# Dilated branch: the first head's probabilities turned by VectorE squares and a trip through memory instead of by TensorE

## The chip, the cores and the metric

The kernel runs on one core of a Trainium2 chip. The metric is the device time of one execution in microseconds (us); lower is better.

## What is computed

A decoder layer over 1024 tokens of width 1024, in float32. One combined projection feeds three causal mixers (A: forgetting attention, B: sparse attention over the 256 keys that an indexer picks, C: dilated sliding-window attention) and their gates; a last projection, the residual and a norm follow. The change is in branch C:

```
C_GROUPS = ((128, 1), (512, 4), (2048, 16))     # window, dilation; 4 heads of 64 each
logits = q . k * 64**-0.5 - slope * dist         # keys t, t-d, t-2d, ...
lse = logsumexp(logits); p = exp(logits - lse)
o = einsum('bhqj,bqjhd->bqhd', p, v)             # then weighted by the groups' softmax shares
```

## The kernel before, in words

**One plan, five engines.** `build_plan` (line 71) writes one list of steps. Each engine walks the same list and does its part of each step, so the list is also the order of every engine's queue. Semaphores do the rest.

**Fill.** TensorE's time goes mostly to projections. A projection tile is 128 output columns by 1024 tokens; it has two banks of PSUM, bank 0 for tokens 0 to 511 and bank 1 for the rest, and its 8 input chunks come as two weight blocks of four. That makes four *pieces* of 12 matmuls (three for each chunk, since every float32 product is split in a high and a low part): first block into bank 0, first block into bank 1, second block into bank 0, second block into bank 1. After the third piece bank 0 is read out, after the fourth bank 1. The read-out of a q or k tile is one ACT instruction (line 1483, the high part) and then one VectorE instruction (line 1814, the low part), which frees the bank. For dilations 4 and 16 both go through a strided view. A v tile is read out by one VectorE transpose (line 1805). The next tile's first piece needs bank 0 free, its second piece bank 1. The weights are split in high and low two blocks ahead (ACT line 1355, VectorE line 1651), at the first piece of each block.

**Attention.** In branch C a channel is a pair of heads, a *run* is two blocks of 128 queries of one channel. There are 6 channels (two for each group) and 4 runs in each, so 24 runs, numbered 0 to 23 here, and *step* s of the loop in `pair_run` (line 241) is the one in which the logits of run s are made. A step of the plan does, in this order:

- TensorE: the logits of run s (line 1252); the product of probabilities and values ("pv", line 1291) of run s-2; the *turn* of run s-1 (line 1264), which transposes its probabilities in blocks of 128x128 through the identity, up to four blocks into a bank.
- VectorE: bias and row maximum of run s (line 1871). ACT: reads out pv (line 1554), copies the turned blocks from PSUM to the ring `pt` (line 1537), then does the exponentials of run s for both heads (line 1519).
- one bit of the selection that branch B needs later (`pick`, 24 bits within this stage): VectorE works out the next bit and does two counts ("bit", lines 1665 to 1678).
- 1.25 to 1.6 pieces of fill, with the read-out that they make due; then the other half of the counts ("bit_count": two by ACT, line 1560, two by VectorE), then as much fill again.

Banks 2 and 3 are handed out in turn to pv and to the groups of turned blocks. A run's blocks number 3 or 4 for each head in group one, 3 in group two, 2 in group three; a run with more than four blocks over both heads needs two groups, and the second one gets the bank that pv just used.

**Squares.** Branches A and B already turn part of the first head's blocks in another way: VectorE transposes the 32x32 squares inside each block in place (line 1792), ACT's queue stores the result to memory (line 1528), and GpSimd's queue loads it again in four DMAs that put the squares in their places (line 1036). pv then reads these blocks from `ptsa`, `ptsb` or `c_tables`. There ACT does the first head's exponentials in the step "square", before the second head's.

The fill follows a pattern of four steps for each channel. With the next channel's tiles q, k and v of four pieces each, the steps hold: (1st) q, q, q; (2nd) q, k, k; (3rd) k, k, v; (4th) v, v, v. Channel 0's fill and the last channel's differ a little.

Of the kernel before, what the change touches and what calls it, by code (L numbers as in the profile page):

```python
# [21 lines left out]
P = 128  # L22
# [3 lines left out]
TB = T // P  # L26
# [16 lines left out]
COL, at = {}, 0  # L43
# [10 lines left out]
SPL = 3  # L54
EARLY = 1
RATE_B = 0.84
SQUARED = {"a": 8, "b": 4}
LAG = {"a": 3, "b": 2}
PTS = {"c": 4, "a": 4, "b": 3}
RELUS = 3  # L60
IDX_BLOCKS = ((7,), (6,), (5,), (4,), (3, 2))
SHARES = 3
# [1 line left out]
NCH = {"a": 4, "b": 4, "c": 6}  # L64
# [6 lines left out]
def build_plan():  # L71
# [20 lines left out]
    def step(kind, **kw):  # L92
        plan.append((kind, kw))
        return kw
# [128 lines left out]
    def pair_run(runs, before, rate, behind_square={}):  # L223


        n = len(runs)
        br = runs[0][0]["br"]
        by_dma = [br == "b" and br in SQUARED or br == "a" and r[0]["ch"] + 1 < NCH["a"] and runs[s + 1][0]["ch"] + 1 < NCH["a"]
                  for s, r in enumerate(runs)]
        by_dma.append(False)  # L230
        for run, dma in zip(runs, by_dma):
            for x in run:
                x.update(dma=dma, moved={})

        def open_parts(r):

            own = sum(x["W"] // P for x in runs[r])
            return 2 * own - len(runs[r][0]["moved"]) if by_dma[r] else 16

        defer[0] = True  # L240
        for s in range(n + 2):
            for f in before.get(s, []):
                f()
            def logits():
                run, wide = runs[s], sum(x["W"] for x in runs[s])
                slots = 2 if wide > HALF else 1
                first_S, first_L, col = nxt("S", slots), nxt("L", 2 * len(run)), 0
                for k, x in enumerate(run):
                    x.update(slots=slots, S=first_S, L=[first_L + k, first_L + len(run) + k], col=col,
                             last=x is run[-1], run=run, held=runs[s - 1][0] if s else None)  # L250
                    col += x["W"]
                    units_seen.append(x)
                    plan.append(("logits", x))

            def turn(run, groups):
                for g in run[0]["groups"][groups]:
                    g.update(use=ring(), tp=nxt("tp"))
                    unit_of_tp.append(run[0])
                step("turn", unit=run[0], groups=groups)

            between = 1 <= s < n and runs[s - 1][0]["slots"] == 2 and open_parts(s - 1) > 8
            if s < n and not between:
                logits()
            due = [r for r in range(max(s - 3, 0), min(s, n)) if r + (LAG[br] if by_dma[r] and by_dma[r + 1] else 2) == s]
            for r in due:
                pv = ring()
                for x in runs[r]:
                    x["pv"] = pv
                    plan.append(("pv", x))

            def square():
                if not by_dma[s]:
                    return
                own = [(x["b"], 0, c) for x in runs[s] for c in range(x["W"] // P)]
                at = len(squares) - 2
                for x in runs[s]:
                    x.update(square=len(squares), single=sum(y["slots"] == 1 for y in squares),
                             moved={part: k for k, part in enumerate(own[:SQUARED[br]])})
                step("square", unit=runs[s][-1], n=len(squares), before=squares[at] if at >= 0 else None)
                squares.append(runs[s][-1])  # L280

            if s < n and not between:
                square()
            for f in behind_square.get(s, []):
                f()
            if 1 <= s <= n:
                moved = runs[s - 1][0]["moved"]
                parts = [(x["b"], hh, c) for x in runs[s - 1] for hh in range(2) for c in range(x["W"] // P)]
                parts = sorted((part for part in parts if part not in moved), key=lambda part: part[1] if moved else 0)
                groups = [dict(parts=parts[g0:g0 + 4]) for g0 in range(0, len(parts), 4)]  # L290
                for x in runs[s - 1]:
                    x["groups"] = groups
                if between:
                    turn(runs[s - 1], slice(0, 2))
                    logits()
                    square()
                    turn(runs[s - 1], slice(2, None))
                else:
                    turn(runs[s - 1], slice(0, None))
            if s == n and runs[0][0]["br"] != "c":  # L300
                step("share_inverse", br=runs[0][0]["br"])
            if s < n:
                plan.append(("exp", runs[s][-1]))
            x = runs[min(s, n - 1)][-1]
            many = len(runs[min(s, n - 1)])
            if s < n and x["br"] == "a" and x["ch"] == NCH["a"] - 1 and x["b"] in (5, 6):
                step("q_split", ch=0, half=x["b"] - 5)
            if s < n and x["br"] == "b" and x["ch"] and x["b"] == 1:
                step("q_split", ch=x["ch"], half=1)
            if s < n and x["br"] == "b" and x["ch"] + 1 < NCH["b"] and x["b"] == 6:  # L310
                step("q_split", ch=x["ch"] + 1, half=0)
            if x["br"] == "b" and s == 0:
                next(fill[0])
                owed[0] = 0.5
            elif x["br"] == "c" and s == n:
                pick(now=False)
                pump(1)
                flush_later()
                count_now()
            elif x["br"] != "b" and s >= n:  # L320
                pump(1 if s == n else 0)
            elif x["br"] == "a" and x["ch"] == NCH["a"] - 1:
                pump(0 if x["b"] == 4 else 1)
            elif x["br"] == "c" and x["ch"] in (0, NCH["c"] - 1):
                pick(now=False)
                pump(1.25 if x["ch"] == 0 else 1.375)
                flush_later()
                count_now()
                pump(1.25 if x["ch"] == 0 else 1.375)
            elif x["br"] == "c":  # L330
                pick(now=False)
                pump(2 * rate)
                flush_later()
                count_now()
                pump(2 * rate)
            else:
                pump(3 if s >= n else many * 2 * rate)
            flush_later()
        defer[0] = False
# [227 lines left out]
def hybrid_layer_kernel(nc, x, norm_g, w_in, b_forget, g_cq, w_uq, w_uq_idx, g_ckv, w_ukv, w_a, w_b, w_c, w_o, final_g,  # L567
# [3 lines left out]
    with ExitStack() as ctx:  # L571
# [55 lines left out]
        v_index = {(a["br"], a["ch"]): a["n"] for kind, a in plan if kind == "v_store"}  # L627
        PR = {"a": at(28, "pa", [P, 2, T]), "b": at(32, "pb", [P, 2, T])}
        PT = {br: at(k, f"pt{br}", [P, PTS[br], 4, P]) for br, k in (("c", 54), ("a", 36), ("b", 40))}
        PTQ = {"a": [at(k, f"ptsa{k}", [P, TB, P]) for k in (44, 76)], "b": [at(46, "ptsb", [P, 4, P])]}  # L630

        idle_out, ties = at(96, "idle_out", [P, T], BF16), at(96, "ties", [P, T], F16)
        idle_out8, state = at(71, "idle_out8", [P, 6 * P], U8), at(71.75, "state", [P, 10, PICKS], I32)
# [697 lines left out]
        def _(act):  # L1331
# [4 lines left out]
            def then(ins):  # L1336
                chain[0] += 1
                ins.then_inc(act_chain, 1)
                act.wait_ge(act_chain, chain[0])

            def split_high(upto):

                while done[0] < min(upto, len(blocks)):
# [20 lines left out]
            for kind, a in plan:  # L1364
# [119 lines left out]
                elif kind == "logits":  # L1484
                    if a["br"] == "c" and a["b"] == 0:
# [7 lines left out]
                        for hh in range(2):  # L1493
                            A(bmc[:, hh, 0:m.shape[1]], m, ACTF.Copy,
                              scale=float(np.float32(c_slope(2 * a["ch"] + hh)) * np.float32(C_GROUPS[g][1]))
                              ).then_inc(bias_ready, 1)
                elif kind == "square":
                    u = a["unit"]
                    if a["n"]:
                        act.wait_ge(square_stored, 16 * a["n"])  # L1500
# [8 lines left out]
                elif kind == "exp":  # L1509

                    if a["held"] is not None:
                        full(act, a["held"]["groups"][-1]["use"])
                        if a["held"]["dma"] and not a["dma"]:
                            act.wait_ge(square_stored, 16 * (a["held"]["square"] + 1))
                    for hh in range(1 if a["dma"] else 0, 2):
                        act.wait_ge(logit_ready, a["L"][hh] + 1)
                        for x in a["run"]:
                            mx, dn = stats_of(x, hh)
# [1 line left out]
                                    scale=-1.0, accum_out=dn)  # L1520
                        if hh or a["slots"] == 2:
                            ins.then_inc(slot_free, 1)
                    if a["dma"]:
                        n, br, W = a["square"], a["br"], len(a["moved"]) * P
                        act.wait_ge(squared, n + 1)
                        if n >= 2:
                            act.wait_ge(square_in[n % 2], 64 * (n // 2))
                        act.dma_start(square_dram[n % 2][0:W // P].rearrange("b p c -> p b c"),
                                      PR[br][:, 0, 0:W].rearrange("p (b c) -> p b c", c=P)).then_inc(square_stored, 16)
                elif kind == "turn":  # L1530
                    u = a["unit"]
                    for grp in u["groups"][a["groups"]]:
# [94 lines left out]
        def _(dve):  # L1627
# [62 lines left out]
            for kind, a in plan:  # L1690
# [94 lines left out]
                elif kind == "square":  # L1785
                    u = a["unit"]
                    W = len(u["moved"]) * P
                    if u["slots"] == 2:
                        dve.wait_ge(slot_free, u["S"] + 1)
                    else:  # L1790
                        dve.wait_ge(single_exp, u["single"] + 1)
# [259 lines left out]
```

## Time and profile before

| | |
|---|---|
| median of 3 runs | 1348.22 us (1348.14 to 1348.27) |
| the profiled execution | 1348.53 us, of which the span is 1346.7 us |
| granted TensorE clock, mean | 0.999 |
| TensorE busy | 1326.0 us, 98% |
| stage of branch C in the trace | 136.4 to about 387 us from the span's start |

In the timeline a row gives the start, the duration, the engine, the line, the tiles, and in brackets how long the engine had sat idle and what ended that. PE is TensorE's matmul row, PEld its weight load, which runs beside the matmul before it; DVE is VectorE; ACTq and POOLq are the DMA issues of ACT and GpSimd. A matmul's duration holds its whole way through the array, so matmuls overlap: the pace is read from the starts.

### The profile page before, as it was taken

The page shows a single profiled execution, that of the slowest core. Times are in us where ns is not written, and L with a number is a line of the kernel's source. Part 1 is how long each engine was busy: PE and PEld are TensorE (multiplying, and loading weights), DVE is VectorE, ACT ScalarE, POOL GpSimd, SP SyncE. Part 2 cuts the span into 40 slices and gives each one's busy share as a digit, 9 for nine tenths or more (in the row PEclk, how much of TensorE's full clock was granted, in tenths as well). Part 3 has the DMA queues.
Part 4 walks back from the last instruction along what each step waited for, and adds up shares of the span by engine and source line. Part 5 has one row for each costly group of instructions (what it writes and reads, how often), then busy time and mean ns, then how long its engine had stood idle before and what let it go on. Part 6 is the DMA issues. An engine that isn't in the chain of part 4 may idle for free.

```text
span 1346.7 us, 20780 instructions
## 1 busy us (share of the span) xinstructions
PE 1326.0 (98%) x7690; PEld 1082.1 (80%) x7690; DVE 771.0 (57%) x1716; ACT 629.4 (47%) x1381; POOL 264.1 (20%) x423
## 2 busy tenths in 40 slices
PE   7999999999999999999999999999999999999998
PEld 6988888777878888887788777787878788888886
DVE  6569866766766875565555555744445354233534
ACT  7467766766754541113443465644454322213223
POOL 3123211002103100003344313323332220000000
PEclk9999999999999999999999999999999999999999
DMA  7054222122214322225555423433544352222522
GB/s 227 24 141 126 71 63 72 50 53 73 72 41 119 99 64 82 80 72 163 162 153 155 141 87 105 127 92 84 156 127 124 119 161 55 78 78 63 188 100 96
DMA packets 146052, 139.54 MB, mean 104 GB/s; under 512 B 13888, under 2 KB 124096, under 8 KB 145696
## 3 DMA queue, kind: packets, MB, share of 16 engines
q0 software_dynamic: 22896, 67.42, 16.9%
q1 hardware_dynamic: 97824, 58.22, 16.0%
q10 hardware_dynamic: 25232, 12.59, 3.2%
q8 instruction: 62, 1.02, 0.3%
q14 instruction: 38, 0.31, 0.1%
HBM read 99.95 MB, written 34.03 MB: 99 GB/s over the span
## 4 chain that ended last, share of the span: by engine, by line
PE 95%; DVE 2%; ACT 1%; issue 1%; POOL 1%; DMA 0%; ACTq 0%; POOLq 0%; DVEq 0%
PE bank L1118 23%; PE bank L1120 23%; PE bank L1119 23%; PE bank L1291 6%; PE slot L1252 6%; PE bank L1264 5%; PE slot L1118 2%; PE slot L1119 2%; PE slot L1120 2%; PE slot L1226 1%; PE bank L1131 0%; DVE slot L1871 0%; ACT yc L1554 0%; DMA iq_st<-iq_hl 0%; PE bank L1177 0%
## 5 line engine op out<-in xcount | busy, mean ns | idle before, releaser
L1118 PE MATMUL bank<-hs,w_hl 128*128 128x512 f32 x1088 | 431.5, 397 | 0.7 <-DVE qa L1814 0.7
L1120 PE MATMUL bank<-hs,w_hl 128*128 128x512 f32 x1088 | 424.3, 390 | 0.0
L1119 PE MATMUL bank<-hs,w_hl 128*128 128x512 f32 x1088 | 423.8, 390 | 0.0
L1651 DVE TENSOR_TENSOR w_hl<-w_raw,w_hl 128x512 fp32r<-128x512 f32 (+1 forms) x168 | 113.6, 678 | 220.7 <-ACT w_hl L1355 219.2
L1120 PEld LDWEIGHTS bank<-hs,w_hl 128*128 128x128 f32 x1088 | 204.2, 188 | 44.0
L1118 PEld LDWEIGHTS bank<-hs,w_hl 128*128 128x128 f32 x1088 | 204.3, 188 | 43.6 <-issue 3.4
L1119 PEld LDWEIGHTS bank<-hs,w_hl 128*128 128x128 f32 x1088 | 204.6, 188 | 39.6
L1355 ACT ACTIVATE w_hl<-w_raw 128x512 fp32r<-128x512 f32 (+1 forms) x168 | 103.9, 621 | 165.1 <-PE bank L1120 155.9
L1678 DVE TENSOR_SCALAR_CACHE_REDUCE idle_out<-score,state 128x768 uint8<-128x768 f32 (+3 forms) x140 | 115.0, 822 | 4.0
L1871 DVE CUSTOM_DVE_ANT_0 slot<-slot,score 128x128 f32<-128x128 f32 (+5 forms) x64 | 47.0, 786 | 50.1 <-PE slot L1252 50.0
L1560 ACT ACTIVATE idle_out<-score,state 128x896 bf16<-128x896 f32 x64 | 69.9, 1093 | 10.0 <-DVE state L1674 8.8
L1036 POOL DMA_DIRECT2D ptsa<-square_scratch x68 | 48.3, 718 | 91.6 <-PE bank L1291 68.8
L1602 ACT ACTIVATE tm<-bank 128x512 f32<-128x512 f32 x46 | 27.5, 598 | 72.3 <-PE bank L1120 72.2
L1036 POOL DMA_DIRECT2D ptsb<-square_scratch x48 | 31.1, 654 | 79.4 <-DMA square_scratch<-pb 68.2
L1036 POOL DMA_DIRECT2D c_tables<-square_scratch x48 | 30.8, 648 | 65.9 <-DMA square_scratch<-pb 65.9
L1849 DVE SCALAR_TENSOR_TENSOR score<-relu_t,nat,score 128x1024 f32<-128x1024 f32 (+5 forms) x42 | 37.9, 947 | 5.0 <-ACT relu_t L1468 4.5
L1870 DVE TENSOR_TENSOR slot<-slot,tri_b 128x128 f32<-128x128 f32 x64 | 20.5, 320 | 33.7 <-PE slot L1252 33.1
L1519 ACT ACTIVATE share_b<-slot,c_tables 128x128 f32<-128x128 f32 (+1 forms) x96 | 38.6, 421 | 1.1 <-DVE c_tables L1871 0.9
L1871 DVE CUSTOM_DVE_ANT_0 slot<-slot,negc 128x128 f32<-128x128 f32 (+7 forms) x48 | 36.8, 766 | 1.7
L1291 PE MATMUL bank<-pta,va 128*64 128x128 f32 x376 | 36.6, 277 | 1.1 <-ACT pta L1537 1.1
L1554 ACT ACTIVATE yb<-bank 128x128 f32<-128x128 f32 (+1 forms) x24 | 7.5, 313 | 64.3 <-PE bank L1291 64.2
L1118 PE MATMUL bank<-ych,w_hl 128*128 128x512 f32 x96 | 37.3, 389 | 0.0
(338 smaller groups left out, 2415.1 us busy)
## 6 DMA issues: line engine op xcount, KB each, us to landing
w_raw<-in_w_in_dram SPq DMA_DIRECT2D x136, 256.0 KB, 2.9
merged_scratch<-ms POOLq DMA_DIRECT2D x16, 512.0 KB, 3.5
ms<-merged_scratch POOLq DMA_DIRECT2D x16, 512.0 KB, 4.0
square_scratch<-pb ACTq DMA_DIRECT2D x20, 256.0 KB, 2.3
xn<-in_x_dram SPq DMA_DIRECT2D x8, 512.0 KB, 6.6
iq_st<-iq_hl POOLq DMA_DIRECT2D x32, 128.0 KB, 2.8
w_raw<-in_w_o_dram SPq DMA_DIRECT2D x16, 256.0 KB, 4.0
v_scratch<-vtc POOLq DMA_DIRECT2D x6, 512.0 KB, 3.1
```

Of the source, the lines that this page charges most:

```text
L1036: pool.dma_start(PTQ[br][n % 2][32 * j:32 * j + 32, 0:W // P, :].rearrange("a b (i c) -> a (b i) c", i=4), mid[0:W // P, :, 32 * j:32 * j ...
L1118: pe.matmul(out_, wh, mh, start=start, stop=False)
L1119: pe.matmul(out_, wh, ml, start=False, stop=False)
L1120: return pe.matmul(out_, wl, mh, start=False, stop=stop)
L1252: ins = pe.matmul(slot_of(a, hh)[1][:, c0:c1], qt[qp][rows, tq], kt[kp][rows, first + c0:first + c1], start=n == 0, stop=n == 2)
L1264: ins = pe.transpose(bank[grp["use"][0]][:, j * P:(j + 1) * P], PR[u["br"]][:, row, at_col:at_col + P], ident[:])
L1291: ins = pe.matmul(bank[a["pv"][0]][cols, out], values, turned, start=c == 0, stop=c == n - 1)
L1355: A(dst, src, ACTF.Copy).then_inc(w_high, 1)
L1560: A(idle_out[:, 0:W], score_of(j + 2), ACTF.Sign, bias=cand[:, j:j + 1].bitcast(F32), scale=-1.0, accum_out=val[:, j:j + 1]).then_inc(act_ ...
L1651: v.tensor_tensor(lo, src, hi.bitcast(F32), ALU.subtract).then_inc(w_low, 1)
L1678: return v.tensor_scalar(idle_out8[:, 0:W] if W <= 6 * P else idle_out[:, 0:W], score_of(j + 2), cand[:, j:j + 1].bitcast(F32), None, op, ...
L1871: v.tensor_tensor_reduce(o, o, logit_bias(x, hh), -slope, 0.0, ALU.add, ALU.min, stats_of(x, hh)[0]).then_inc(logit_ready, 1)
```

## The change

In branch C, every run but the last has its first head's blocks (all of them, at most 4: 3, 4, 4, 4 in each channel of group one, 3 in group two, 2 in group three) turned by squares. The step "square" is not made where the other branches have it but behind `pick`, so after VectorE's first two counts, and a step "square_store" follows it at once. ACT keeps both heads' exponentials together in "exp"; VectorE's transpose waits for both (`slot_free`); ACT's store waits for the transpose (`squared`). GpSimd's loads stand at the same place in its queue. The ring `pt` of branch C shrinks from 4 to 2, and two tiles for the loaded blocks take its place.

```diff
-SQUARED = {"a": 8, "b": 4}
-LAG = {"a": 3, "b": 2}
-PTS = {"c": 4, "a": 4, "b": 3}
+SQUARED = {"c": 4, "a": 8, "b": 4}
+LAG = {"c": 2, "a": 3, "b": 2}
+PTS = {"c": 2, "a": 4, "b": 3}
...
-        by_dma = [br == "b" and br in SQUARED or br == "a" and r[0]["ch"] + 1 < NCH["a"] and runs[s + 1][0]["ch"] + 1 < NCH["a"]
+        by_dma = [br == "c" and s + 1 < n or br == "b" and br in SQUARED or br == "a" and r[0]["ch"] + 1 < NCH["a"] and runs[s + 1][0]["ch"] + 1 < NCH["a"]
...
-                step("square", unit=runs[s][-1], n=len(squares), before=squares[at] if at >= 0 else None)
+                if br != "c":
+                    step("square", unit=runs[s][-1], n=len(squares), before=squares[at] if at >= 0 else None)
+                else:
+                    moving.append(lambda: step("square", unit=runs[s][-1], n=runs[s][0]["square"],
+                                               before=squares[at] if at >= 0 else None))
...
             elif x["br"] == "c":
                 pick(now=False)
+                for f in moving:
+                    f()
+                if moving:
+                    step("square_store", unit=runs[s][-1])
+                moving.clear()
                 pump(2 * rate)
                 flush_later()
                 count_now()
...
-        PTQ = {"a": [at(k, f"ptsa{k}", [P, TB, P]) for k in (44, 76)], "b": [at(46, "ptsb", [P, 4, P])]}
+        PTQ = {"c": [at(k, f"ptsc{k}", [P, 4, P]) for k in (58, 60)], "a": [at(k, f"ptsa{k}", [P, TB, P]) for k in (44, 76)], "b": [at(46, "ptsb", [P, 4, P])]}
...
+            def store_square(u):
+
+                n, br, W = u["square"], u["br"], len(u["moved"]) * P
+                act.wait_ge(squared, n + 1)
+                if n >= 2:
+                    act.wait_ge(square_in[n % 2], 64 * (n // 2))
+                act.dma_start(square_dram[n % 2][0:W // P].rearrange("b p c -> p b c"),
+                              PR[br][:, 0, 0:W].rearrange("p (b c) -> p b c", c=P)).then_inc(square_stored, 16)
...
-                elif kind == "square":
+                elif kind == "square" and a["unit"]["br"] != "c":
...
-                        if a["held"]["dma"] and not a["dma"]:
+                        if a["held"]["dma"] and (not a["dma"] or a["br"] == "c"):
                             act.wait_ge(square_stored, 16 * (a["held"]["square"] + 1))
-                    for hh in range(1 if a["dma"] else 0, 2):
+                    for hh in range(1 if a["dma"] and a["br"] != "c" else 0, 2):
...
+                elif kind == "square_store":
+                    store_square(a["unit"])
...
-                    if u["slots"] == 2:
+                    if u["slots"] == 2 or u["br"] == "c":
                         dve.wait_ge(slot_free, u["S"] + 1)
```

## Rows read from the trace of the kernel before

**Rows 1.** The page: busy time by engine, then the chain that ended last, by engine.

```profile
PE 1326.0 (98%) x7690; PEld 1082.1 (80%) x7690; DVE 771.0 (57%) x1716; ACT 629.4 (47%) x1381; POOL 264.1 (20%) x423
...
PE 95%; DVE 2%; ACT 1%; issue 1%; POOL 1%; DMA 0%; ACTq 0%; POOLq 0%; DVEq 0%
```

**Rows 2.** Busy time by engine in branch C's stage, then clock, DMA share, GB/s.

```profile
136.40:386.80 250.40, 249.34 (x1527) 199.23 (x1527) 175.88 (x556) 171.29 (x422) 32.80 (x39) 1.00 0.24 63
```

**Rows 3.** Line 1264: branch C's transposes (duration ns min/median/max), an idle cause.

```profile
L1264 PE MATMUL bank<-ident,share_b x140: 272/273/332, 143.9 to 386.9; 128*128 128x128 f32 x140
...
  ACT yc L1554: 3.2, 10
```

**Rows 4.** Timeline, weight loads: turns in steps 3, 14, 18 and what follows.

```profile
163.12 0.97 PEld L1264 LDWEIGHTS bank<-ident,share_b 128*128 128x128 f32 x8 [0.17 <-issue]
164.06 0.19 PEld L1118 LDWEIGHTS bank<-hs,w_hl 128*128 128x128 f32 x1
...
285.53 0.42 PEld L1264 LDWEIGHTS bank<-ident,share_b 128*128 128x128 f32 x4 [0.17 <-issue]
286.33 0.20 PEld L1264 LDWEIGHTS bank<-ident,share_b 128*128 128x128 f32 x2 [0.39 <-ACT yc L1554]
286.50 0.19 PEld L1118 LDWEIGHTS bank<-hs,w_hl 128*128 128x128 f32 x1
...
328.93 0.42 PEld L1264 LDWEIGHTS bank<-ident,share_b 128*128 128x128 f32 x4 [0.17 <-issue]
329.32 0.19 PEld L1118 LDWEIGHTS bank<-hs,w_hl 128*128 128x128 f32 x1
```

**Rows 5.** Branch B: VectorE's squares; ACT's store and its next instruction.

```profile
L1792 DVE STREAM_TRANSPOSE pb<-pb x24: 578/712/714, 829.2 to 1056.0; 128x512 f32<-128x512 f32 x20, 128x384 f32<-128x384 f32 x4
...
829.83 0.37 ACTq L1528 DMA_DIRECT2D square_scratch<-pb  x1
830.29 1.09 ACT L1580 ACTIVATE tm<-bank 128x512 f32<-128x512 f32 x2 [0.30 <-issue]
```

**Rows 6.** Timeline, step 9: last early count, read-out of q, next use of the bank.

```profile
231.03 0.19 PEld L1118 LDWEIGHTS bank<-hs,w_hl 128*128 128x128 f32 x1
...
234.01 0.08 DVE L1678 DVE_READ_ACCUMULATOR idle_out<-score,state 128x1 f32 x1
...
234.10 1.10 ACT L1483 ACTIVATE qc<-bank 128x512 fp32r<-128x512 f32 x1 [0.62 <-PE bank L1120]
...
235.31 1.10 DVE L1814 SCALAR_TENSOR_TENSOR qc<-bank,qc 128x512 fp32r<-128x512 f32 x1 [1.21 <-ACT qc L1483]
...
236.52 0.19 PEld L1118 LDWEIGHTS bank<-hs,w_hl 128*128 128x128 f32 x1 [0.16 <-issue]
```

**Rows 7.** Timeline, step 6: end of the exponentials, weight split, read-out of k.

```profile
199.96 0.22 ACT L1519 ACTIVATION_READ_ACCUMULATOR share_b<-slot,c_tables 128x1 f32 x1
200.05 0.65 ACT L1355 ACTIVATE w_hl<-w_raw 128x512 fp32r<-128x512 f32 x1
200.57 1.14 ACT L1483 ACTIVATE kc<-bank 128x512 fp32r<-128x512 f32 x1
...
201.74 1.08 DVE L1814 SCALAR_TENSOR_TENSOR kc<-bank,kc 128x512 fp32r<-128x512 f32 x1 [0.24 <-ACT kc L1483]
...
202.93 0.19 PEld L1118 LDWEIGHTS bank<-hs,w_hl 128*128 128x128 f32 x1 [0.16 <-issue]
```

**Rows 8.** Landing of store and load, GpSimd's issues, the values' load, step 2's pv.

```profile
square_scratch<-pb ACTq DMA_DIRECT2D x20, 256.0 KB, 2.3
...
ptsb<-square_scratch POOLq DMA_DIRECT2D x48, 64.0 KB, 2.4
...
L1036 POOL DMA_DIRECT2D ptsb<-square_scratch x48: 649/652/697, 838.7 to 1062.6; - x48
...
142.65 3.97 POOL L1027 DMA_DIRECT2D vc<-v_scratch  x4 [2.64 <-DMA v_scratch<-vtc]
...
153.77 0.64 PEld L1291 LDWEIGHTS bank<-ptc,vc 128*64 128x64 f32 x12
```

More of the change, by code:

```diff
@@ L238, in open_parts @@
             return 2 * own - len(runs[r][0]["moved"]) if by_dma[r] else 16
+        moving = []
         defer[0] = True
@@ L276, in square @@
                 for x in runs[s]:
-                    x.update(square=len(squares), single=sum(y["slots"] == 1 for y in squares),
+                    x.update(square=len(squares), single=sum(y["slots"] == 1 and y["br"] != "c" for y in squares),
                              moved={part: k for k, part in enumerate(own[:SQUARED[br]])})
-                step("square", unit=runs[s][-1], n=len(squares), before=squares[at] if at >= 0 else None)
+                if br != "c":
[3 more added lines that the diff above has]
+                                               before=squares[at] if at >= 0 else None))
                 squares.append(runs[s][-1])
@@ L331, in pair_run @@
                 pick(now=False)
+                for f in moving:
+                    f()
+                if moving:
+                    step("square_store", unit=runs[s][-1])
+                moving.clear()
                 pump(2 * rate)
@@ L1522, in _ @@
                             ins.then_inc(slot_free, 1)
[L1523 to L1529, printed above, removed]
+                    if a["dma"] and a["br"] != "c":
+                        store_square(a)
+                elif kind == "square_store":
+                    store_square(a["unit"])
                 elif kind == "turn":
```

## The prediction

> **What bounds the kernel now.** I read the page first: TensorE is busy for 98% of the span and holds 95% of the chain that ended last [rows 1]. The stretches give the same for branch C's stage alone: of 250.4 us TensorE is busy for 249.3, at full clock, VectorE for 176, ACT for 171 [rows 2]. So what leaves TensorE's queue in this stage is worth its full time, and what comes to VectorE (70%) and ACT (68%) costs nothing by its sum, only by where it stands. The timeline then shows how close those two are. In step 9, ACT begins to read out q's last half when its piece is done, at 234.10; VectorE ends the low part at 236.41; TensorE starts on that bank at 236.52 [rows 6]. The piece between is 12 matmuls in 2.73 us, the read-out takes 2.31 us and the crossings: no slack. Step 6 has the same in k's third piece: read-out from 200.57 to 202.82, next use at 202.93 [rows 7]. Both are strided read-outs, 1.1 us on each engine. They stand in two steps of each channel whose fill makes a q and k for dilation 4 or 16: steps 5, 9, 13, 17 (q, as in rows 6) and 6, 10, 14, 18 (k, as in rows 7). I call these the eight tight steps; in all of them the read-out comes first behind the place where the change puts its new work.
>
> **What leaves TensorE.** Of 140 transposes [rows 3], 68 go: 3+4+4+4 blocks in each of two channels, 3 in 8 runs, 2 in 7 (the last run keeps its own). Their price is not the 273 ns of the row but their pace. A turn of eight takes 0.94 us from its first load to the next block's, one of six with a wait for pv's bank in the middle 0.97, one of four in a single group 0.39 [rows 4]: about 0.10 us for each block, and some 0.15 to 0.5 for the second group and its wait (rows 3 has ten such waits, 3.2 us). Afterwards every run has one group: 4 blocks 0.39, 3 blocks 0.30, 2 blocks 0.20. So a step gains 0.55 where eight become four (6 steps), 0.67 where six with the wait become three (7 steps), about 0.4 where six without it do (steps 1, 5, 9; step 1's, a little shorter, 0.3), 0.19 where four become two (7 steps). Sum 3.3 + 4.7 + 1.15 + 1.3 = **10.5 us**. The Trainium skill (TensorE: Matmul & The Clock Gate, Part 4: PE-mode transpose) gives a transpose some 275 ns inside a kernel. The duration in rows 3 agrees, but the starts in rows 4 do not make it a cost; by it the cut would be an estimated 68 x 0.275 = 18.7 us.
>
> **What comes to ACT and VectorE.** ACT loses 16 copies of a second group (0.38 to 0.60 us each); its exponentials, which follow them, end some 0.5 us earlier in steps 6, 10 and 14. VectorE gets 23 transposes: 0.71 us at 512 columns, 0.58 at 384 [rows 5], and by that slope 0.44 at 256. ACT gets a wait for each, 0.04 us of crossing, the issue of the store, 0.37, and 0.09 until its next instruction [rows 5]. Rows 5 is the only place where another instruction follows close; the bounds are 0 (the issue slips under ACT's work, as it does where an exponential runs) and 0.5. I take 0.5, since here ACT has nothing running: it is waiting.
>
> *Tight steps of q.* Step 9: the count ends at 234.09, the squares (384) at 234.70, ACT is free at 235.20 instead of reading from 234.10. The read-out ends 2.31 later, 237.51, and TensorE takes the bank at 237.62, not at 236.52: **1.10 us later than before**, although the turn ahead of it became shorter. The same sum from the same rows of the other three: step 5 1.48 (512 columns, and the count ends late), step 13 1.12, step 17 1.34 (here the piece was done 0.4 us before the count). Together 5.04.
>
> *Tight steps of k.* Step 6: the exponentials end at 200.18, without the second copy at 199.6; squares to 200.35, ACT free at 200.85; the weight split that was at 200.05 and the read-out 0.52 behind it move to 201.4 instead of 200.57, TensorE to 203.75 instead of 202.93: 0.82 later. Steps 10 and 14 (384 columns; the read-out waited 0.3 for its piece before) 0.33 each, step 18 0.66. Together 2.1.
>
> So in eight steps 7.2 us are lost instead of 3.8 gained, and the other fifteen turns keep 6.7. Net **+0.5 us**.
>
> **What costs nothing, and its cover.** *The loads.* The store goes out at most 7.2 us into a step, lands after 2.3, GpSimd issues 4 x 0.65, the last lands 2.4 later [rows 8]: 14.5 us. pv of that run comes two steps on, about 22 us later. The least slack is at run 0: its loads queue behind the values' load, which ends at 146.6, land near 151.7, and pv starts at 153.8 [rows 8], or 153.5 once the turn is shorter. GpSimd's values' store is ready to go well after the previous run's loads; its values' load moves at most behind them and is needed two steps on. *The wait before pv* has been met by then; branches A and B have the same wait and start pv as closely behind the logits. *Non-strided read-outs* take 1.3 us, so 1.4 are free there (step 21: 0.1 left after the delay). *Behind the delay* in step 5: ACT's counts and weight split end near 194.9 (3.3 before its next work), VectorE's split near 195.8, 1.5 before step 6's maxima. *DMA*: 8.9 MB more within 250 us at a share of 0.24 [rows 2]. Weights are loaded three blocks ahead.
>
> **The rivals.** *Faster: the read-outs are not late.* If ACT's new wait cost nothing at the tight steps (or half of it), the whole cut stays: 1348.2 - 10.5 = 1337.7, with half the loss 1343. For it speaks only that the eight delays are sums of small crossings; against it the order of the queue, in which ACT cannot start the read-out before the store, and the store not before the squares. Chance 0.2. The case of the skill's price, 18.7 less 7.2, would give 1336.7; rows 4 leave it 0.02, taken in here.
>
> *Slower: the delay is carried on.* The one pair that comes in sequence is q's step and k's step. If VectorE's work behind the late read-out (two counts and a weight split) ended more than the 1.5 us slack after the next logits, that step's maxima, exponentials and squares would all start late, and the k read-out, already last, would pass it on one to one. Place: steps 6, 10, 14, 18. It decides from a delay of 1.5 us above the 1.1 to 1.5 that I find; each 1 us beyond costs 4 us, so 1352.7. For it: step 5 is long already; against: the step itself grows by the same delay, which gives the slack back. Chance 0.1. *Slower: the loads come late.* They would need 7.5 us more than the rows give (a landing of 4 us instead of 2.4 would cost run 0 alone some 1.5 us); each 1 us beyond costs up to 20. Chance 0.05.
>
> **How the numbers follow.** The profiled execution took 1348.53 us, 1.8 more than its span and 0.3 above the median of the three runs; I put the difference on the median: 1348.2 + 0.5 = **1348.7**. Two tenths of a percent, about what a measurement of this kernel can tell from no change, is 2.7 us. My forecast (chance 0.65) holds as long as neither the cut nor the loss is off by more than some 2.5 us; with the store's issue at its lower bound 0 the loss falls by 3.7 (1345), and were ACT's exponentials not to move up it grows by 1.7 (1350.4). The range takes in both and half of the faster rival: 1343.0 to 1351.5. Faster by over 0.2%: 0.25 (the rival and an edge of the forecast), slower by over 0.2%: 0.15, within: 0.6.
>
> **What would show it.** TensorE's transposes in the stage 72 instead of 140, each turn one group, no wait for yc within a turn; steps 7, 8, 11, 12, 15, 16 shorter by 0.55 to 0.68. In the eight tight steps a new idle time of TensorE, 0.8 to 1.9 us, ended by VectorE's line 1814, with ACT's line 1483 starting 0.5 us behind a transpose of line 1792; TensorE's busy time in the stage down by some 10 us with the stage as long as before. I am wrong if these gaps are missing or below 0.5 us, or if TensorE waits at line 1291 for the loads.

## The result, and the profile after

The changed kernel takes **1350.12 us** (median of 20 runs, 1349.78 to 1351.12) against 1348.24 (20 runs, 1347.97 to 1349.18) for the kernel before: a ratio of 1.0015, 95% interval 1.0008 to 1.0022. That is inside the 0.2% that counted as no change, and 1.4 us above the forecast of 1348.7. The interval lies above 1: the kernel is a little slower, by 1.9 us, and not exactly as fast. A tie could have many causes, so what follows asks whether it is the one that was forecast: some 10 us off TensorE, and as much given back in waits.

In the new file the lines have moved: the fill's matmuls 1118 to 1120 are 1133 to 1135, the turn 1264 is 1279, pv 1291 is 1306, the logits 1252 are 1267, the read-out 1483 and 1814 is 1507 and 1835, the v read-out 1805 is 1826, the weight split 1355 and 1651 is 1379 and 1672, the early count 1678 is 1699, the squares 1792 are 1813, the late counts of ACT 1560 are 1581, and the store is 1362.

The page of the kernel after: busy time by engine, and the chain that ended last (against [rows 1]).

```profile
PE 1318.2 (98%) x7622; PEld 1074.3 (80%) x7622; DVE 782.5 (58%) x1739; ACT 618.7 (46%) x1365; POOL 319.9 (24%) x515
...
PE 86%; DVE 7%; ACT 4%; issue 3%; POOL 1%; ACTq 0%; DMA 0%; DVEq 0%; POOLq 0%
```

TensorE's busy time is down by 7.8 us, though the kernel is no shorter. The chain of waits shows where the time went: TensorE's share fell from 95% to 86%, and VectorE and ACT, which held 3% together, hold 11%.

The same stretch as in [rows 2]; then, from the view of one line, the transposes of branch C (as [rows 3]).

```profile
136.40:386.80 250.40, 240.17 (x1442) 190.45 (x1439) 186.79 (x576) 160.82 (x405) 88.65 (x131) 1.00 0.38 98
```

```profile
L1279 PE MATMUL bank<-ident,share_b x72: 272/273/333, 143.3 to 388.4; 128*128 128x128 f32 x72
```

In the stage TensorE is busy for 240.2 instead of 249.3 us of 250.4. 9.2 us of work are gone and 10.2 us of idle time stand there, where 1.1 stood before. (The stretch is fixed in time; the stage's last step begins 1.7 us later than before.) The clock is at 1.00 in both, so it has no part in this. The 72 transposes are the forecast's; each still lasts 273 ns.

What ended TensorE's waits in the kernel after (total us, times, longest).

```profile
PE bank L1133 <- DVE qc L1835: 5.2, 4, 1.5
PE bank L1133 <- DVE kc L1835: 3.0, 4, 1.1
PE bank L1133 <- DVE vtc L1826: 1.4, 1, 1.4
...
PE bank L1133 <- DVE kc_low L1835: 0.6, 1, 0.6
```

The four waits for q are the tight steps 5, 9, 13 and 17. Of the four for k three are the tight steps 6, 10 and 14, and the fourth, 0.37 us, stands in step 3; the last row, for the low half of the last channel's k, is tight step 18. So the eight tight steps hold 8.5 us, each ended by the low half of the read-out. What is not in the forecast is the wait in step 3 and the one for a v tile's read-out, in step 4: 1.8 us together.

The timeline of the kernel after, step 9, against [rows 6].

```profile
234.85 0.08 DVE L1699 DVE_READ_ACCUMULATOR idle_out<-score,state 128x1 f32 x1
234.97 0.58 DVE L1813 STREAM_TRANSPOSE share_b<-share_b 128x384 f32<-128x384 f32 x1
235.58 0.37 ACTq L1362 DMA_DIRECT2D square_scratch<-share_b  x1
235.99 1.09 ACT L1507 ACTIVATE qc<-bank 128x512 fp32r<-128x512 f32 x1 [1.93 <-DVE share_b L1813]
237.12 1.04 DVE L1835 SCALAR_TENSOR_TENSOR qc<-bank,qc 128x512 fp32r<-128x512 f32 x1 [1.57 <-ACT qc L1507]
238.27 0.19 PEld L1133 LDWEIGHTS bank<-hs,w_hl 128*128 128x128 f32 x1 [1.49 <-issue]
```

This is the chain of the prediction, link by link. The count ends at 234.93, the squares take 0.58, the store is issued 0.03 behind them and takes 0.37, ACT begins the read-out 0.04 later. ACT has by then sat idle for 1.93 us. In [rows 6] the read-out began 0.01 behind the count's end, here 1.06. The bank is free so late that TensorE idles for 1.49 us.

Step 6, for k (against [rows 7]).

```profile
201.60 0.37 ACTq L1362 DMA_DIRECT2D square_scratch<-share_b  x1
202.07 0.63 ACT L1379 ACTIVATE w_hl<-w_raw 128x512 fp32r<-128x512 f32 x1 [1.31 <-DVE share_b L1813]
...
204.88 0.19 PEld L1133 LDWEIGHTS bank<-hs,w_hl 128*128 128x128 f32 x1 [1.54 <-issue]
```

Here a weight split stands between the store and the read-out and is pushed along with it.

The step table below is worked out from the timelines: the length of a step (first load of its logits to the next step's) less its length before, in us, and TensorE's longest idle time behind the turn. Steps 7, 8, 11, 12, 15, 16 and 19 to 23 are taken together.

```
step                        1     2     3     4  |   5     6     9    10    13    14    17    18 | others
forecast                 -0.3 -0.55 -0.55 -0.55  | 1.48  0.82  1.10  0.33  1.12  0.33  1.34  0.66 | -4.8
after                   -0.16 -0.57  0.08  1.05  | 1.29  0.84  0.89  0.29  0.90  0.26  1.18  0.66 | -4.45
idle                     0.29    -   0.58  1.61  | 1.88  1.54  1.49  1.10  1.81  1.13  1.61  1.04 |
```

Sum: 0.40 + 6.31 - 4.45 = 2.26 us. The profiled execution itself took 1349.78 us (span 1348.0), 1.25 above that of before: its stage begins 0.55 us earlier, before anything of the change has run, and what follows the stage takes 0.45 less. The medians differ by 1.9.

### The profile page after: what moved, and what is told of

Read it like the earlier page. It is cut to its first block, busy times and chain, and to the rows that moved or that the text cites. A ratio compares the mean times of both kernels' runs of the same rounds, so it can differ in the third digit from the quotient of the medians.

```text
span 1348.0 us, 20807 instructions
## 1 busy us (share of the span) xinstructions
PE 1318.2 (98%) x7622; PEld 1074.3 (80%) x7622; DVE 782.5 (58%) x1739; ACT 618.7 (46%) x1365; POOL 319.9 (24%) x515
## 4 chain that ended last, share of the span: by engine, by line
PE 86%; DVE 7%; ACT 4%; issue 3%; POOL 1%; ACTq 0%; DMA 0%; DVEq 0%; POOLq 0%
PE bank L1133 21%; PE bank L1135 21%; PE bank L1134 21%; PE bank L1306 6%; PE slot L1267 6%; PE bank L1279 4%; PE slot L1133 2%; PE slot L1134 2%; PE slot L1135 2%; DVE slot L1892 1%; DVE score L1870 1%; DVE idle_out L1699 1%; ACT qc L1507 1%; DVE qc L1835 1%; DVE share_b L1813 1%
## 5 line engine op out<-in xcount | busy, mean ns | idle before, releaser
L1051 POOL DMA_DIRECT2D ptsc<-square_scratch x92 | 59.2, 759 | 128.3 <-DMA square_scratch<-share_b 128.0
L1125 POOL DMA_DIRECT2D merged_scratch<-ms x8 | 4.8, 602 | 145.7 <-DVE ms L2012 145.7
```

Of the source, the lines that this page charges most:

```text
L1051: pool.dma_start(PTQ[br][n % 2][32 * j:32 * j + 32, 0:W // P, :].rearrange("a b (i c) -> a (b i) c", i=4), mid[0:W // P, :, 32 * j:32 * j ...
```

## The experiments

**Theory one** (the prediction's): the cut is real and is taken back because ACT's wait and its store stand ahead of read-outs that have no slack. **Theory two**: it is the added work that costs, VectorE's squares and the memory traffic, wherever it stands. **Theory three**, which the table suggested: the first steps lose for another reason than the tight ones. Each time below is a median, beside the kernel before on the same chip.

### The store alone, behind the read-out

In both orders of branch C the step "square_store" moves behind the fill and its read-out. VectorE's squares stay where they are.

```diff
                 for f in moving:
                     f()
+                pump(2 * rate)
+                flush_later()
                 if moving:
                     step("square_store", unit=runs[s][-1])
                 moving.clear()
-                pump(2 * rate)
-                flush_later()
                 count_now()
```

> ACT's wait for the squares and its store stand behind the read-out that the first half of the fill makes due, instead of ahead of it; VectorE's squares stay where they are. Theory one (the loss is ACT's wait ahead of the read-outs of q and k): TensorE's eight gaps of 1.0 to 1.9 us go, those steps get shorter than before the change by 0.2 to 0.7 us each instead of longer by 0.3 to 1.3; with the backlog of channel 0 at least halved the time is 1338 to 1340.5 us. Theory two (VectorE's squares in front of the low part of the read-out hold TensorE up, wherever ACT waits): the gaps stay at half their size or more, 1345 us or above.

Measured: 1338.27 us against 1348.18, ratio 0.9927 (0.9898 to 0.9956). The same kernel, run more often:

> The kernel with ACT's store behind the read-out again, timed closely: 1338.0 to 1338.8 us, 9.5 to 10 us below the kernel before.

Measured: **1338.33 us** (1337.71 to 1338.59) against 1348.28, ratio 0.9926 (0.9912 to 0.9939). The timeline of the first set, step 9:

```profile
229.45 1.11 ACT L1507 ACTIVATE qc<-bank 128x512 fp32r<-128x512 f32 x1 [0.45 <-PE bank L1135]
229.91 0.58 DVE L1813 STREAM_TRANSPOSE share_b<-share_b 128x384 f32<-128x384 f32 x1
230.52 0.37 ACTq L1362 DMA_DIRECT2D square_scratch<-share_b  x1
230.60 1.10 DVE L1835 SCALAR_TENSOR_TENSOR qc<-bank,qc 128x512 fp32r<-128x512 f32 x1
```

ACT reads out as soon as TensorE is done. VectorE turns the squares while ACT makes the high part of q, time in which VectorE had to wait anyway ([rows 6]: 1.21 us of idle time before its low part), and the store goes out behind. The same stretch as in [rows 2], for this kernel:

```profile
136.40:386.80 250.40, 250.27 (x1508) 200.35 (x1505) 192.17 (x598) 168.56 (x415) 89.78 (x132) 1.00 0.39 100
```

TensorE idles for 0.13 us. (By 386.80 this kernel has left the stage some 10 us ago, so the row holds a piece of what follows too.) All 24 steps together are 10.16 us shorter than before, so nearly the whole cut reaches the end; what is missing stands in step 4, which gains 0.23 instead of 0.55. The same squares, stores, loads and bytes as in the change cost next to nothing here, so theory two falls for VectorE's squares at this place and for the memory traffic. This is also the best version found; it beats both kernels.

### The squares where A and B have them

The kernel before with branch C simply added to the tables: ACT does the first head's exponentials first, VectorE's squares come at once, ACT's store follows the second head's exponentials, ahead of `pick`.

```diff
-SQUARED = {"a": 8, "b": 4}
-LAG = {"a": 3, "b": 2}
-PTS = {"c": 4, "a": 4, "b": 3}
+SQUARED = {"c": 4, "a": 8, "b": 4}
+LAG = {"c": 2, "a": 3, "b": 2}
+PTS = {"c": 2, "a": 4, "b": 3}
...
-        by_dma = [br == "b" and br in SQUARED or ...
+        by_dma = [br == "c" and s + 1 < n or br == "b" and br in SQUARED or ...
...
-        PTQ = {"a": ...
+        PTQ = {"c": [at(k, f"ptsc{k}", [P, 4, P]) for k in (58, 60)], "a": ...
```

> The squares as branches A and B have them: first head's exponentials, VectorE's squares ahead of the selection's counts, store behind the second head's exponentials. ACT's wait then lies under its own second pair of exponentials. Theory one: the read-outs are late only by what VectorE's counts move (nothing waits for them) and the store's 0.37 us: 1338 to 1341 us. Theory two: the squares still come ahead of the read-outs on VectorE, 1345 us or above.

Measured: 1340.87 us against 1348.18, ratio 0.9946 (0.9923 to 0.9968). The steps sum to -7.82. What ended TensorE's waits there (this file keeps the line numbers of before):

```profile
PE bank L1118 <- DVE qc L1814: 1.2, 4, 0.4
```

The squares now stand ahead of VectorE's early counts, and ACT goes from its exponentials to the read-out without idle time. What stays is less: idle times of 0.58 to 0.77 us stay in q's four steps and 0.28 to 0.43 in k's. In step 9 it is VectorE's queue that holds them:

```profile
230.04 1.11 ACT L1483 ACTIVATE qc<-bank 128x512 fp32r<-128x512 f32 x1
...
231.74 1.08 DVE L1814 SCALAR_TENSOR_TENSOR qc<-bank,qc 128x512 fp32r<-128x512 f32 x1
```

ACT's high part is done by 231.15, but VectorE is in its early counts until 231.70: they stand behind the squares, which came at 229.02. So added work of VectorE does cost here, a few tenths of a microsecond a step, where it pushes the counts into the read-out. Steps 1 to 4 gain all that was forecast, -0.31, -0.56, -0.55 and -0.57.

### GpSimd's queue stores

ACT neither waits nor stores. GpSimd waits for the squares, issues the store and then, as before, the loads.

```diff
                 if br == "c":
+                    pool.wait_ge(squared, n + 1)
+                    if n >= 2:
+                        pool.wait_ge(square_in[n % 2], 64 * (n // 2))
+                    pool.dma_start(square_dram[n % 2][0:W // P].rearrange("b p c -> p b c"),
+                                   PR[br][:, 0, 0:W].rearrange("p (b c) -> p b c", c=P)).then_inc(c_stored, 16)
+                    pool.wait_ge(c_stored, 16 * (n + 1))
...
-                elif kind == "square_store":
-                    store_square(a["unit"])
```

> GpSimd's queue issues the store as well as the loads, ACT has neither wait nor issue; VectorE's squares stay behind the first two counts. Theory one: all eight gaps go, 1337.5 to 1340 us, the cut of 10.5 us. Theory two: the gaps stay, 1345 us or above. The loads land about 1 us later than with ACT's store, still 6 us ahead of their use.

Measured: 1342.8 us against 1348.18, ratio 0.9958 (0.9942 to 0.9974). The tight read-outs are free again (steps 9 and 10: -0.44, -0.69), but the time is above the 1337.5 to 1340 expected, and not all loads were 6 us ahead of their use, as had been expected. GpSimd's queue, in order, around step 17:

```profile
302.13 0.58 POOL L1037 DMA_DIRECT2D v_scratch<-vtc  x1
306.39 0.96 POOL L1044 DMA_DIRECT2D vc<-v_scratch  x1 [3.69 <-DMA v_scratch<-vtc]
307.53 2.93 POOL L1044 DMA_DIRECT2D vc<-v_scratch  x3 [0.17 <-issue]
309.86 1.30 POOL L1055 DMA_DIRECT2D square_scratch<-share_b  x1
314.86 2.32 POOL L1061 DMA_DIRECT2D ptsc<-square_scratch  x4 [3.70 <-DMA square_scratch<-share_b]
...
314.65 0.37 ACT L1556 ACTIVATE share_b<-slot,c_tables 128x128 f32<-128x128 f32 x1 [2.33 <-DMA square_scratch<-share_b]
```

VectorE had turned run 16's squares by 304.08. GpSimd was then waiting for the values' store, and their loads stand ahead of the new one, so it went out 5.8 us late. ACT's exponentials of the next run write the tile that is being stored and waited 2.33 us for it. The same order stands in every channel; it costs most in steps 13, 17 and 21 (+0.04, +1.11, +1.38, idle times 0.95 to 1.69). In step 2 pv waited for the load, as TensorE's waits show:

```profile
PE bank L1316 <- DMA ptsc<-square_scratch: 1.3, 1, 1.3
```

So a step moved to another engine's queue took on that queue's waits. For the same reason the loads, for which the prediction found a least slack of 1.8 us at run 0, come late as soon as something stands ahead of them.

### ACT waits, GpSimd stores

As the last one, but ACT waits for the squares where the change has it. This parts the wait from the issue.

```diff
                 elif kind == "square_store":
-                    store_square(a["unit"])
+                    act.wait_ge(squared, a["unit"]["square"] + 1)
```

> As the run in which GpSimd stores, but ACT still waits for VectorE's squares at the place of the store. It splits the loss at the eight tight steps in the wait and the issue. By the sum of the prediction the issue with what follows is 0.46 us of each delay and the rest the wait: the gaps shrink by 0.46 us each, 3.7 us in all, to about 1346.3 us. If the issue slips under the wait or the semaphore, 1350 us; if the issue is the whole loss, 1338 to 1340.

Measured: 1351.56 us against 1348.18, ratio 1.0023 (1.0012 to 1.0034). As a total this lies outside all three expected values (1346.3, 1350, 1338 to 1340), since GpSimd's queue brings waits of its own: step 21 alone is 3.91 longer than before the change, step 2 0.71. In the tight steps 5 and 17 ACT's exponentials waited 1.6 us for the late store, so they tell nothing here (step 5 is even 0.21 longer than in the change). The other six tight steps have no such wait:

```
step                         6     9    10    13    14    18
after                     0.84  0.89  0.29  0.90  0.26  0.66
ACT waits, no issue       0.37  0.50 -0.20  0.50 -0.16  0.26
difference                0.47  0.39  0.49  0.40  0.42  0.40
```

The issue of the store costs 0.39 to 0.49 us where an engine stands ready behind it, for which the prediction took 0.46 (0.37 and 0.09). The wait costs the rest. Step 9 of this kernel:

```profile
235.55 1.11 ACT L1517 ACTIVATE qc<-bank 128x512 fp32r<-128x512 f32 x1 [1.53 <-DVE share_b L1826]
```

ACT starts here as soon as the squares end (the row's releaser), after 1.53 us of idle time instead of 1.93.

### TensorE keeps the tight runs

```diff
-        by_dma = [br == "c" and s + 1 < n or ...
+        by_dma = [br == "c" and s + 1 < n and s not in (5, 6, 9, 10, 13, 14, 17, 18) or ...
```

> As the change, but the eight runs of the tight steps (5, 6, 9, 10, 13, 14, 17, 18) keep all their blocks on TensorE: no squares, no wait and no store in those steps. Theory one: in these steps TensorE's gaps go and ACT's queue is as before the change, so they last as long as before or a little less; the 6.3 us that they add now are gone and the other steps keep what they gain: 1343 to 1345 us. Theory two (the loss comes from something common to the stage, the traffic of the loads or GpSimd's work): a third of it goes at most, 1348 us or above.

Measured: 1344.56 us against 1348.31, ratio 0.9973 (0.9962 to 0.9984). The eight idle times are gone (all at most 0.21, as before), at the price of the cut of eight turns. Steps 1 to 4 are as in the change (-0.16, -0.56, +0.05, +1.07): their loss has nothing to do with the tight steps. Step 21, a lone step behind a v tile, is even longer than in the change (+0.38 against +0.06).

### One block instead of four

```diff
-SQUARED = {"c": 4, "a": 8, "b": 4}
+SQUARED = {"c": 1, "a": 8, "b": 4}
```

> As the change with one block of each run moved instead of two to four: 23 blocks instead of 68, waits and stores in the same number and place. Theory one (the wait and the issue cost, not the amount moved): the squares of 128 columns take about 0.3 us instead of 0.44 to 0.71, so each tight step still is about 0.7 us late, while the turns gain only 0.1 us for each block and most keep their second group: 1350 to 1353 us, no faster than the whole change. A loss in proportion to what is moved would give 1348.5 to 1349.

Measured: 1353.52 us against 1348.31, ratio 1.0035 (1.0019 to 1.0051), a little above the upper end expected (1353). A quarter to a half of the data is moved, and the kernel is **slower** than the change: the eight tight steps still lose 5.18 us (6.31 with all blocks), steps 2, 3 and 21 are longer by 0.56, 0.28 and 0.35, and the turns of most other steps gain only some 0.1. The loss comes per wait and issue, the gain per block.

### Squares and store both behind the read-out

The first experiment left the squares ahead of the read-out. Here both follow it.

```diff
+                pump(2 * rate)
+                flush_later()
                 for f in moving:
                     f()
                 if moving:
                     step("square_store", unit=runs[s][-1])
                 moving.clear()
-                pump(2 * rate)
-                flush_later()
                 count_now()
```

> VectorE's squares too stand behind the read-out, so that nothing new is ahead of it on either engine; ACT's wait then comes ahead of its two counts. If VectorE's squares cost nothing where they are (they fit in the 1 us in which it waits for ACT's high part), this gives nothing more: 1338 to 1339 us, and 1340 or above if the later stores bring loads too late for pv in the short steps of channel 0. If the squares ahead of the low part cost something, 1337.5 us or below.

Measured: 1341.57 us against 1348.28, ratio 0.995 (0.9936 to 0.9963). The tight steps are as clean as in the first experiment. Of the 3.2 us between the two, 2.9 stand in steps 1 and 4, which are 0.67 and 1.74 us longer than before the change. The time falls among those expected if the loads came late, but not for that reason: no row has TensorE waiting for `ptsc`. The end of step 3 and the start of step 4 there, then TensorE's wait:

```profile
171.24 0.37 ACTq L1362 DMA_DIRECT2D square_scratch<-share_b  x1
171.65 1.04 ACT L1581 ACTIVATE idle_out<-score,state 128x896 bf16<-128x896 f32 x1 [1.99 <-DVE share_b L1813]
...
176.26 0.19 PEld L1133 LDWEIGHTS bank<-hs,w_hl 128*128 128x128 f32 x1 [2.29 <-DVE w_hl L1672]
```

```profile
PE bank L1133 <- DVE vtc L1826: 2.1, 1, 2.1
```

Where no read-out comes first, ACT's late counts, the weight split and VectorE's v read-out stand behind the wait, and they have little slack there too. The clean tight steps show that the squares ahead of the low part, as in the first experiment, cost nothing there.

### Channel 0 by TensorE

```diff
-        by_dma = [br == "c" and s + 1 < n or ...
+        by_dma = [br == "c" and 4 <= s and s + 1 < n or ...
```

> As the change, but the first channel's four runs keep all blocks on TensorE. If the 1.1 us that steps 3 and 4 lost against a forecast gain of 1.1 come from ACT's waits in channel 0 carried from step to step, steps 1 to 4 last as before the change (together 0.4 us less than in the change), the eight gaps stay: 1349.3 to 1350 us. If they come from elsewhere, steps 3 and 4 stay long and the time goes up by the gain given up in steps 1 and 2: 1350.8 us or above.

Measured: 1349.84 us against 1348.28, ratio 1.0011 (1.0002 to 1.0020). Steps 1 to 4 are as long as before (0.00, 0.00, +0.01, 0.00), and the eight tight steps lose what they lose in the change, 6.34 us. The median is 0.3 below the change's, as 0.4 in the table would have it. So the two losses are independent of each other, and channel 0's squares, which by the turns should have given 1.95 us, cost the change 0.4.

## Why the prediction was right, and where it was off

**The cut, 10.5 us: right.** With the store out of the way the steps are shorter by 10.16 us, and 9.9 to 10.0 arrive in the time. The price by pace holds to 3% (steps 7, 8: -0.55 and -0.57; 11, 12, 15, 16: -0.69 to -0.73; 19, 20, 22: -0.19). The price by duration, for which the Trainium skill (TensorE: Matmul & The Clock Gate, Part 4: PE-mode transpose) was cited, would have made it an estimated 18.7. The row agrees with its 275 ns (273), and it is still no cost: transposes overlap, eight of them taking 0.94 us in [rows 4] and not 2.2. The 1336.7 that the prediction works out from 18.7 is wrong as a sum: its 7.2 already holds the turns of the tight steps. The other fifteen steps have 45 of the 68 blocks, 12.3 us at 273 ns, and 12.3 less 7.2 makes 1343.1. The pace decides against both.

**The tight steps, 7.2 us lost: right in place, sign and cause, 6.3 in size.** All eight gaps are there, 1.0 to 1.9 us, ended by VectorE's low part, and they vanish when only the store moves. The steps of k came out within 0.07 us each; those of q are 0.16 to 0.22 below, in all four. In step 9 the time from the count's end to ACT's start is 1.06 us (0.04, 0.58, 0.03, 0.37, 0.04) instead of the 1.11 taken, and the read-out itself 2.17 instead of 2.31: VectorE begins 1.13 behind ACT, not 1.21, and takes 1.04, not 1.10. ACT's issue was priced at 0.37 + 0.09; here 0.04 followed it in step 9, 0.10 in step 6.

**Steps 1 to 4: wrong, and the main miss, 2.35 us.** The step of the prediction that failed is the sentence on cover, "non-strided read-outs take 1.3 us, so 1.4 are free there": it looked at one read-out in one step. In channel 0 the delay does not end with its step; step 2 is 7.75 us long. ACT's waits for the squares in steps 1 to 3:

```profile
151.60 0.63 ACT L1379 ACTIVATE w_hl<-w_raw 128x512 fp32r<-128x512 f32 x1 [2.39 <-DVE share_b L1813]
...
161.41 0.60 ACT L1507 ACTIVATE kc<-bank 128x512 fp32r<-128x512 f32 x1 [1.99 <-DVE share_b L1813]
...
170.58 1.04 ACT L1581 ACTIVATE idle_out<-score,state 128x896 bf16<-128x896 f32 x1 [1.99 <-DVE share_b L1813]
```

Some two microseconds of idle time stand in each step ahead of ACT's splits, read-outs and counts. The timelines show that the delay is handed on. Behind the first load of a step's logits, ACT's first exponential comes after 4.85, 5.33 and 6.74 us in steps 1, 2 and 3, where it came after 3.70, 3.45 and 3.67 before: 1.1, 1.9 and 3.1 us late, more in each step. With channel 0's turns left to TensorE (the last experiment) it comes after 3.49, 3.45 and 3.67, so nothing else brings the delay. For step 3, whose logits begin at 159.91 (161.19 before), that exponential and ACT's last weight split, first after and then before:

```profile
166.65 0.47 ACT L1543 ACTIVATE share_b<-slot,c_tables 128x256 f32<-128x256 f32 x1 [0.93 <-DVE c_tables L1892]
...
173.02 0.63 ACT L1379 ACTIVATE w_hl<-w_raw 128x512 fp32r<-128x512 f32 x1
```

```profile
164.86 0.47 ACT L1519 ACTIVATE share_b<-slot,c_tables 128x256 f32<-128x256 f32 x1
...
169.11 0.63 ACT L1355 ACTIVATE w_hl<-w_raw 128x512 fp32r<-128x512 f32 x1
```

The split is 5.2 us late, 3.1 of it brought along and 2.1 from step 3's own wait and store. VectorE's half of the split and its v read-out follow it, and TensorE pays with 0.58 in step 3 (for k's low half) and 1.61 in step 4:

```profile
174.36 1.31 DVE L1826 STREAM_TRANSPOSE vtc<-bank 128x512 f32<-128x512 f32 x2
175.19 0.19 PEld L1133 LDWEIGHTS bank<-hs,w_hl 128*128 128x128 f32 x1 [1.61 <-DVE w_hl L1672]
```

The load's row names VectorE's split; the matmul behind it waited until the first of the two v transposes had freed its bank (the 1.4 us of the waits above). This is the mechanism of the rival "the delay is carried on", in a place that the rival did not name: it was put at k's steps, which took no more than forecast. The store's place accounts for most of it: behind the read-out, the same four steps gain 1.64 of the forecast 1.95.

**Step 21**: "0.1 left" was a slack too small to call; TensorE idled for 0.39 and the step is 0.06 longer instead of 0.19 shorter. With the steps above: 0.5 forecast, - 0.9 for the tight steps, + 2.35, + 0.3 for step 21 and rounding, gives the 2.26 of the table.

**The loads: right.** No row of the change has TensorE waiting at pv for `ptsc`. The store lands after 1.8 to 2.3 us, the loads after 2.2 to 2.5. The experiments with GpSimd's queue show how thin the cover was.

The time came out near because the two large terms were each within 1 us, and in part by luck: the terms that were held to cost nothing added 2.7 us in the table, and the tight steps gave 0.9 of it back. Without that the table would stand some 3.1 us above the kernel before, beyond the 2.7 that counted as no change. The tie was not a change that does nothing, and one line's place decided 12 us.

## What to carry to other kernels

When a DMA is issued from a compute engine's queue, the wait ahead of it is that engine's wait: place it behind the work that frees the bottleneck's buffers, and not as early as its data allow. If a cut leaves the bottleneck and the time stays, look at its idle times and at what stands ahead of the instruction that ends them, before giving up the cut: here moving one step took the time from 1350.1 to 1338.3 us. Check the cover of a delay over a run of steps, where queues are fullest, and not for one instruction alone.

## What the runs showed of the hardware

A DMA issue on ACT's queue holds back the instruction behind it by its own 0.37 us and 0.04 to 0.10 more, as the experiment that left it out confirms (0.39 to 0.49 a step). In all 23 stores of branch C in the change the addition has one of two sizes: 0.05 ahead of a read-out or a count, 0.10 ahead of a weight split.

Stores of the same size took longer from GpSimd's queue than from ACT's. The DMA issues of the kernel after, then of GpSimd storing with ACT free, then with ACT waiting (KB each, us to landing):

```profile
square_scratch<-share_b ACTq DMA_DIRECT2D x10, 192.0 KB, 2.1
```

```profile
square_scratch<-share_b POOLq DMA_DIRECT2D x10, 192.0 KB, 3.8
```

```profile
square_scratch<-share_b POOLq DMA_DIRECT2D x10, 192.0 KB, 2.5
```

The stores of 128 and 256 KB have the same order: 1.8 and 2.3 us, 3.4 and 3.9, 2.3 and 2.7. Some of it is the issue itself, 0.77 us instead of 0.37. Why the two kernels with GpSimd's stores differ by 1.1 to 1.3 us stays open.

GpSimd's issues are also not of one length. The loads of the change took 0.58 to 1.43 us each:

```profile
L1051 POOL DMA_DIRECT2D ptsc<-square_scratch x92: 582/621/1425, 145.1 to 376.7; - x92
```

```profile
147.99 0.30 DVE L1688 TENSOR_SCALAR state<-state 128x6 f32<-128x6 f32 x1
```

The first is the view of line 1051, the second a row of the timeline: in the time of one of the long issues a six-element operation of VectorE took 0.30 us, where its neighbours took 0.17. Which holds up which is open.
